# First stages of a two-block fp32 kernel reordered: inputs in pieces, weight splits inside the recurrent branch's chain

## What is computed

```python
h = rms_norm(x, norm1_g)                       # x: 256 x 1024
proj = h @ w_in                                # 1024 x (1792 + 1536 + 512 + 3072)
p_rwkv, p_sb, q_mem, gate_logits = split(proj)

# recurrent branch: token shift, low-rank rates and gate, normalised keys, recurrence
p = p + (prev(p) - p) * mu
r, k, v, wl, al, gl = split(p)
decay = exp(-exp(-softplus(-(w0 + tanh(wl) @ w2)) - 0.5))
a = sigmoid(a0 + al @ a2)
g = sigmoid(gl) @ g2
kk = (k * k_k) / max(norm_of_head(k * k_k), 1e-12)
k = k * (1 + (a - 1) * k_a)
y_a = (norm(recurrence(r, decay, k, v, kk, a)) + bonus(r, k, r_k) * v) * g

# stick-breaking attention branch, 8 heads
q, k, v = split(p_sb); q = rms_norm(q, q_g); k = rms_norm(k, k_g)
y_b = stick_breaking_attention(q, k, v)

# memory branch, 4 heads
mk, mv = split(rms_norm(mem, mem_g) @ w_mem_kv)
y_m = softmax(norm(q_mem) @ norm(mk).T) @ mv
```

## Time and profile before

| | us |
|---|---|
| median of 3 runs | 1236.6 (1236.52 to 1238.52) |
| the profiled execution | 1236.65 |
| its span in the profile | 1234.5 |
| PE busy within the span | 1174.4 (95%) |
| DVE / ACT / POOL busy | 898.0 / 658.2 / 358.9 |
| mean granted clock of PE | 0.991 |

### The profile page before, as it was taken

How to read it: one execution, slowest core, us unless ns; L and a number is a source line. 1 busy time by engine, 2 the same in 40 slices (tenths; PEclk the granted TensorE clock), 3 DMA queues, 4 the chain that set the end, 5 groups by cost and what they waited for, 6 DMA issues and landing times.

```text
span 1234.5 us, 24680 instructions
## 1 busy us (share of the span) xinstructions
PE 1174.4 (95%) x9392; PEld 1090.1 (88%) x9392; DVE 898.0 (73%) x1297; ACT 658.2 (53%) x964; POOL 358.9 (29%) x330
## 2 busy tenths in 40 slices
PE   5987998999999999999999799999999989999998
PEld 5976867988999999988888799999898779999987
DVE  5777656437568899976747688888677758988963
ACT  4575772225445555554466565555444665555542
POOL 3343102000002455511202334552127122555500
PEclk9999999999999999999999899999999999999999
DMA  7633320035656555555452355555554415555552
GB/s 261 217 120 115 120 69 2 4 104 170 188 181 203 182 179 178 177 185 186 153 179 92 119 167 179 180 177 187 184 177 136 144 45 188 172 184 172 186 185 73
DMA packets 53699, 188.77 MB, mean 153 GB/s; under 512 B 6000, under 2 KB 6128, under 8 KB 53232
## 3 DMA queue, kind: packets, MB, share of 16 engines
q1 hardware_dynamic: 52016, 182.47, 46.4%
q10 hardware_dynamic: 1600, 5.12, 1.2%
HBM read 186.52 MB, written 1.05 MB: 152 GB/s over the span
## 4 chain that ended last, share of the span: by engine, by line
PE 81%; DVE 9%; ACT 7%; issue 2%; DMA 0%; ACTq 0%; POOL 0%; DVEq 0%
PE psA L456 71%; PE psB L456 10%; DVE rounded L1680 3%; ACT arena L1096 3%; ACT rounded L1096 2%; DVE arena L1680 2%; DVE arena L1683 2%; ACT L1096 2%; DVE rounded L1683 1%; DMA arena<-in_par 0%; DVE arena L2008 0%; DVE arena L1776 0%; DVE arena L2155 0%; DVE arena L1707 0%; DVE arena L2057 0%
## 5 line engine op out<-in xcount | busy, mean ns | idle before, releaser
L456 PE MATMUL psA<-rounded,rounded 128*128 128x256 f32 (+1 forms) x7440 | 1017.9, 299 | 40.5 <-DVE rounded L1680 19.6
L456 PEld LDWEIGHTS psA<-rounded,rounded 128*128 128x128 f32 x7440 | 961.8, 193 | 91.6 <-issue 27.1
L1680 DVE TENSOR_TENSOR rounded<-arena,rounded 128x1024 fp32r<-128x1024 f32 (+1 forms) x357 | 447.5, 1274 | 85.3 <-ACT rounded L1096 81.2
L1096 ACT ACTIVATE rounded<-arena 128x1024 fp32r<-128x1024 f32 (+1 forms) x441 | 387.4, 924 | 217.5 <-PE psA L456 73.9
L1505 POOL TENSOR_TENSOR arena<-arena 128x256 f32<-128x256 f32 (+1 forms) x123 | 163.7, 1337 | 620.7 <-ACT arena L1096 247.0
L1096 ACT ACTIVATE arena<-arena 128x256 f32<-128x256 f32 (+6 forms) x272 | 143.3, 562 | 179.6 <-DVE arena L1680 135.8
L1683 DVE SCALAR_TENSOR_TENSOR arena<-arena 128x255 f32<-128x255 f32 (+4 forms) x334 | 171.1, 555 | 36.7 <-ACT arena L1096 26.6
L456 PE MATMUL psB<-arena 64*64 64x64 f32 (+11 forms) x1816 | 154.9, 274 | 10.5 <-DVE arena L1680 6.9
L456 PEld LDWEIGHTS psB<-arena 64*64 64x64 f32 (+5 forms) x1816 | 113.9, 151 | 41.1 <-issue 20.9
L1680 DVE TENSOR_TENSOR arena<-arena,psA 128x256 f32<-128x256 f32 (+1 forms) x84 | 38.4, 457 | 71.7 <-PE psA L456 47.8
L1595 POOL TENSOR_TENSOR rounded<-arena,rounded 128x256 f32 (+1 forms) x63 | 86.5, 1373 | 10.0 <-POOL rounded L1593 8.8
(11 more groups left out here) (70 smaller groups left out, 170.7 us busy)
## 6 DMA issues: line engine op xcount, KB each, us to landing
arena<-in_w SPq DMA_DIRECT2D x344, 512.0 KB, 3.5
arena<-in_x SPq DMA_DIRECT2D x2, 512.0 KB, 6.1
arena<-in_mem ACTq DMA_DIRECT2D x2, 512.0 KB, 5.9
arena<-in_x ACTq DMA_DIRECT2D x1, 1024.0 KB, 6.4
arena<-in_con ACTq DMA_DIRECT2D x1, 1024.0 KB, 5.9
out<-arena SPq DMA_DIRECT2D x1, 1024.0 KB, 3.9
arena<-in_con ACTq DMA_DIRECT2D x1, 992.0 KB, 5.0
arena<-in_par ACTq DMA_DIRECT2D x1, 264.0 KB, 3.1
```

Of the source, the lines that this page charges most:

```text
L456: ins_ = nc.tensor.matmul(o, l, r, start=start, stop=stop, skip_group_check=shared)
L1096: return nc.scalar.activation(o, i, f, **kw)
L1680: return V.tensor_tensor(o, a, b, op)
```

## The change

- **Start.** ACT loads the parameters first and the constants behind the split of slot 0. A copy of one column stands between the wait for the parameters and the first split. Slot 0 comes in two halves with a semaphore each (`w0a`, `w0`), x in three pieces (2, 2 and 4 chunks); ACT and DVE split slot 0 half by half, and PE waits for the first half only. DVE does its small `omm` operation behind `xgL` instead of before the split. POOL's squares of x wait for all of x and for all of `xgL`.
- **Loop over rw.** DVE makes the chunks of h one unit earlier (`H_AT`), ACT copies each pair one unit after DVE made it, behind the splits and the multiplication of that unit. On ACT and DVE the splits of slots 16 and 17 move to the end of this loop.
- **Behind the loop.** PE does `kn` first, then the rates' first half, the first half of `sk0`, the rates' second half and the gate, and the second half of `sk0`. The banks of psB are taken in that order. On DVE the `kn` maxima come before the scan; on both engines splits of slots 18 to 26 stand at fixed places between the steps of the chain.
- **Memory branch.** POOL's subtractions for `h_m` wait for `fm` 3. `mk0` is done in two halves (slot 30, slot 31): z0 to z3, first half, z4 to z7, second half. ACT splits slots 34 and 35 before the exponential of the scores instead of behind it.
- Semaphores of the constant loads and of two memsets are merged; this changes no order of work.

```diff
-SM = (["rx", "rm", "dl0", "al0", "dl1", "al1", "gl0", "gl1", "kn0", "kn1",
+SM = (["rx", "rm", "kn0", "kn1", "dl0", "al0", "dl1", "al1", "gl0", "gl1",
...
-        H_AT = ((), (0,), (1,), (2, 3), (4, 5), (6, 7), ())
+        H_AT = ((), (0, 1), (2, 3), (4, 5), (6, 7), (), ())
+        X_AT = ((0, 2), (2, 4), (4, 8))
...
-            slot(0, 0)
-            for n in range(2):
+            for n, name in enumerate(("w0a", "w0")):
                 c = slice(4 * n, 4 * n + 4)
-                sp.dma_start(xT[:, c, :], ins["x"][:, c, :]).then_inc(sem(f"ld_x{n}"), 16)
+                sp.dma_start(ring[0].rearrange("p (a n) -> p a n", a=SLOT)[:, c, :],
+                             ins["w"][0:1, :, :].rearrange("a p (b n) -> p (a b) n", b=SLOT)[:, c, :])\
+                    .then_inc(sem(name), 16)
+            for n, (a, b) in enumerate(X_AT):
+                sp.dma_start(xT[:, a:b, :], ins["x"][:, a:b, :]).then_inc(sem(f"ld_x{n}"), 16)
...
-            for u in range(2):
+            def lora_rates(u):
...
             reduce_pairs(["kn0", "kn1"], bones, BN, "kk_sq")
+            lora_rates(0)
+            project_half("sk0", H, 0)
+            lora_rates(1)
+            lora_gate(0)
+            lora_gate(1)
+            project_half("sk0", H, 1)
...
-            project(["sk0", "sk1"], H)
+            project(["sk1"], H)
...
-            for c in range(4):
-                sb_scores(c)
-            project_mem("mk0", True)
+            sb_scores(0)
+            sb_scores(1)
+            project_mem("mk0", True, 0)
+            sb_scores(2)
+            sb_scores(3)
+            project_mem("mk0", True, 1)
...
-            act.dma_start(con1[:, 0:NCON0], ins["con"][:, 0:NCON0]).then_inc(sem("ld_con"), 16)
             act.dma_start(par[:, 0:NPAR1], ins["par"][:, 0:NPAR1]).then_inc(sem("ld_par"), 16)
             act.wait_ge(sem("ld_par"), 16)
+            A(small[:, 126:127], par[:, 0:1], ACT.Copy).then_inc(sem("act_aux"), 1)
+            act.wait_ge(sem("w0a"), 16)
+            A(fr(upper[0][:, 0:512]), ring[0][:, 0:512], ACT.Copy).then_inc(sem("w0a_upper"), 1)
             act.wait_ge(sem("w0"), 16)
-            split_to(1)
+            A(fr(upper[0][:, 512:1024]), ring[0][:, 512:1024], ACT.Copy).then_inc(sem("w_upper"), 1)
+            split[0] = 1
+            act.dma_start(con1[:, 0:NCON0], ins["con"][:, 0:NCON0]).then_inc(sem("ld_con"), 16)
...
-                for k in H_AT[u]:
+                for k in H_AT[u - 1] if u else ():
...
+            split_to(18)
             act.dma_start(wgate, ins["wg"]).then_inc(sem("ld_wg"), 16)
...
-            split_to(21)
-            for name, dst, b in (("dl", SG, "w0"), ("al", AA, "a0")):
-                for u in range(2):
+            def rates(u):
+                for name, dst, b in (("dl", SG, "w0"), ("al", AA, "a0")):
...
+            rates(0)
+            split_to(21)
+            rates(1)
             copy2("gl0", GT[:, 0:2, :])
             copy2("gl1", GT[:, 2:4, :])
+            split_to(22)
             ready(act, "kk_max", 2)
             step(A(KM, KM, ACT.Ln))
             A(KM, KM, ACT.Exp, scale=-0.5).then_inc(sem("kk_inv"), 1)
-            copy2("sk0", sbqk[:, 4:6, :])
-            split_to(SLOT_END["sk1"] + 1)
+            split_to(23)
...
             A(SG, SG, ACT.Exp, scale=-DECAY).then_inc(sem("decays"), 1)
+            copy2("sk0", sbqk[:, 4:6, :])
+            split_to(24)
             copy2("sk1", sbqk[:, 6:8, :])
...
             copy2("mk0", mqk[:, 4:6, :])
+            split_to(SLOT_END["mk1"] + 2)
             sb_exp(0)
...
+            for n in range(len(X_AT)):
+                pool.wait_ge(sem(f"ld_x{n}"), 16)
+            ready(pool, "xg", KD)
             for u in range(4):
-                pool.wait_ge(sem(f"ld_x{u // 2}"), 16)
                 square("x", sqx, xT[:, 2 * u:2 * u + 2, :], u)
...
+            ready(pool, "fm", 3)
             for k in range(KD):
                 ready(pool, "h_m_upper", k + 1)
...
-            ready(pool, "fm", 3)
...
                 if u < 5:
                     scaled(u + 2)
+            split_to(18)
             settle()
...
-            split_to(18)
             dve.wait_ge(*freed("rm"))
             step(V.reciprocal(rstdm, rstdm))
+            split_to(20)
...
-            split_to(SLOT_END["sk0"] + 1)
+            split_to(22)
             ready(dve, "kk_inv")
             step(tt(K1, K1, KM, ALU.mult))
-            split_to(SLOT_END["sk0"] + 2)
+            split_to(23)
             dve.wait_ge(*freed("al1"))
             ready(dve, "decays", 2)
             mark(tt(AR[:, 0:4, :], K1, SG, ALU.mult))
-            pump()
+            split_to(24)
             settle()
             mark(tt(K1, K1, AA, ALU.mult))
             tt(AR[:, 4:8, :], r_, GG, ALU.mult).then_inc(sem("fm"), 1)
-            pump()
+            split_to(25)
             settle()
             tt(K1, K1, LC, ALU.mult).then_inc(sem("fm"), 1)
...
-            pump()
+            split_to(26)
             settle()
-            pump(2)
...
-            pump()
+            split_to(27)
```

90 lines of the change are left out of this document (54 added, 36 removed).

## The result

The changed kernel takes 1229.05 us (median of 4 runs, 1228.51 to 1230.13); the kernel before took 1237.14 beside it. The ratio is 0.9935, 95% interval [0.9923, 0.9947]: 8.1 us faster. The forecast was 13.2 us faster, and 1229.05 lies 0.05 us outside the slow end of its range (1218 to 1229). The profiled execution took 1228.64, with a span of 1226.8.

The account below looks back on a forecast made before the run. PE, busy 95% of the span, was taken as the bound, with time won only where it idles or runs at the lower clock. 6.1 + 2.3 + 3.1 + 5.5 - 3.8 = 13.2 us faster: 1223.4 us, range 1218 to 1229.

Parts of the forecast that it names:

- A: The start, up to `rx`: parameters first and loads in pieces bring `rx` from 28.5 to 22.4; gain 6.1 us, bounds 4.5 and 7.5.
- B: Loop over rw: slot 8 split earlier, PE's wait there 0.8 instead of 2.06; gain 2.3 us, bounds 1.2 and 2.6.
- C: sq0 and sq1: the waits of 0.77 for POOL and 2.31 at slot 16 go; gain 3.1 us, bounds 2.5 and 3.1.
- D: End of sq1 to the scores: 47.7 us instead of 53.2; gain 5.5 us, bounds 2.5 and 7.5.
- E: Scores and mk0: PE waits for DVE before both halves; loss 3.8 us, bounds 5.0 lost and 0.8 gained.
- Rival 1: Scores and mk0: the first half of mk0 starts at once, DVE having slot 30 in time; 1219.4 us, chance 0.13.
- rival 3: The start: pieces land one behind the other, parameters as late as before, PE gains 1 us; 1228.5 us, chance 0.07.
- rival 4: Slots 20 to 26: every split waits for the chain and makes PE wait; slower, 1240.6 us, chance 0.04.
- rival 5: Whole change: order does not matter, waits only move, sum within 2.5 us of nothing; 1235 us, chance 0.03.
- rival 2: Recurrent chain late: slips of 1.3 us at each of slots 23 to 25, two clock drops; 1229.7 us, chance 0.11.

## Why the prediction missed

**A, the step that failed.** 3.07 instead of 6.1, below the bound of 4.5. POOL's work was named as the danger, and a wait of PE in front of `rx` as a sign of being wrong; its price was wrong. I took POOL's squares from 10.3 to 19.7, with the 9.4 us that they took in before. There most of them ran beside DVE's xgL, eight steps of 0.98; here they run beside six splits of 2.04, and took 13.65 us, to 25.13. With them gone rx came at 22.30. The term was a duration carried from one neighbour to another. Before's own timeline had the right price, for the one step of POOL that stood beside a split (DVE's from 8.08 to 9.98); the four behind it, beside xgL, took 1.22 to 1.34:

```profile
8.97 2.13 POOL L1520 TENSOR_TENSOR arena<-arena 128x512 f32<-128x512 f32 x1
```

That the 96 matmuls were done at 22.55 with `rx` forecast at 22.4 is partly luck: PE began 1.26 us later than forecast and needed 14.09 us where the forecast had 15.2. The forecast's own steps (12.3, 0.3, 9.0 and 0.5) make 22.1, and it had put the first matmuls' 0.21 us on the clock, while the profile shows a granted clock of 1.00 over them in both kernels; what makes them slow is not shown.

**B and C.** 2.90 and 3.97, forecast 2.3 and 3.1. The wait at slot 8 is 0.59 (forecast 0.8), those at slot 16 and for POOL are gone, and the run that undoes both parts lost 7.5 at the end. Both gains lie above their bounds (2.6 and 3.1). In B the stretch at half clock was worth more than the 1.0 forecast: the 144 matmuls took 19.00 in before and 17.51 in after. In C I had counted only the idle times: the 96 matmuls took 15.67 less the waits of 0.77 and 2.31, 12.59, in before, and 11.70 in after. From one start to the next PE lost 0.93 at the wait for POOL, 0.43 more at the next four matmuls (held again for POOL's last chunk of h), and 2.54 at slot 16; nearly all others follow at 0.12. A wait cost 0.16 to 0.23 more than the idle time that the profile gives it.

**D, mis-sized.** 3.37 instead of 5.5, inside the bounds. The waits at slots 22 to 25 were 0.38, 1.66, 1.24 and 0.28, 3.56 in all, where I had 2.4. And I looked for what POOL's subtractions would do to the splits that they left, not to what lies where they went: DVE's norms, 4.21 us instead of the 2.7 of before, with slot 29 behind them: 1.48. That slot had no line in my walk.

**E, right in mechanism, 0.85 too small.** Two waits of 2.64 and 2.52 (forecast 2.6 and 2.5). The half clock behind the first added 1.48 (4.60 instead of 3.12), which I had put into the bound only; the rest of the stage was 0.6 better than forecast. Rival 1, that E costs nothing, fell, though two moved calls on DVE make it true.

**What no term had.** Between 148 and 1060 us after gained 1.55, of which some 1.0 is a stretch at half clock that did not come (162 matmuls in 6.17, where the pace of after, 3.07 / 97, makes 5.13). The same wait stands ahead of it in both kernels: before's timeline, a window of before from the last 0.6 us of the wait on (granted clock 0.51), and after's timeline:

```profile
212.00 6.17 PE L456 MATMUL psB<-arena 64*64 64x64 f32 x162 [3.06 <-DVE arena L1680]
```

```profile
211.40:214.80 3.40, 2.80 (x52) 2.80 (x54) 1.83 (x3) 0.00 (x0) 0.00 (x0) 0.51 0.00 0
```

```profile
203.15 3.07 PE L460 MATMUL psB<-arena 64*64 64x64 f32 x97 [3.10 <-DVE arena L1721]
```

Nothing shows this as a gain of the change. At this same wait a stretch at half clock came in nine of the fourteen traces and stayed out in five. From mem's tokens to the third feed-forward the traces took between 911.50 (after) and 913.33 us, and before with one idle copy more needed 911.66, hardly more than after. So the 1.55 is of the size by which executions scatter, and luck in the pair of traces compared.

And the third feed-forward took 2.51. "Every microsecond won early moves all that follows" was the sentence that failed: it holds for waits, not for where instructions lie. Rivals 3 to 5 fell with the runs above. The totals of rivals 3 (1228.5) and 2 (1229.7) both lie within 0.7 us of the result, but neither reason is what happened: the parameters let ACT start at 3.99 instead of 6.99, and the slips at slots 23 to 25 were 0.46, 0.34 and 0, not 1.3 each, with no drop of the clock.

Open: what decides whether the clock falls behind a wait of 3 us was not settled; nor what lies at the late position of ACT's program.

## What to carry to other kernels

When work on POOL is moved, price it beside its new neighbour on DVE, and price the neighbour too: 0.40 or 1.23 to 1.46 us for a cast, 1.2 or 2.04 for a split. When PE's order is changed, walk each feeder's order against it; the halves of mk0 cost 4.6 us against mk0 in one piece, until DVE's two splits went ahead of the scores and made them 1.4 faster than it. And when a loop far from the edit changes its length with every wait unchanged, compare single records for the first late one: an instruction more or less on an engine can be the whole difference, and a few idle copies can take it back.
